# Shift and scale applied to the transposed inputs, per channel, in the first stage of a two-block model kernel

## What is computed

```python
sh1, sc1, gt1, sh2, sc2, gt2 = jnp.split((silu(c) @ w_mod + b_mod)[:, None, :], 6, axis=-1)
csh1, csc1, cgt1, csh2, csc2, cgt2 = jnp.split(silu(c_ctx) @ w_mod + b_mod, 6, axis=-1)
h  = rms_norm(x,   g_pre_mix) * (1.0 + sc1)  + sh1      # 256 latent tokens
hc = rms_norm(ctx, g_pre_mix) * (1.0 + csc1) + csh1     # 256 context tokens
mix, mix_c = token_mix(h, hc, w_in, ...)                # begins with h @ w_in, hc @ w_in
```

## Time and profile before

| | us |
|---|---|
| median of 3 runs | 2170.5 |
| lowest, highest | 2169.6, 2174.39 |
| the profiled execution's own time | 2179.26 |
| its span in the trace | 2177.5 |
| PE busy | 1751.4 |
| DVE busy | 480.1 |
| ACT busy | 352.3 |

### The profile page before, as it was taken

How to read it: one execution, slowest core, us unless ns; L and a number is a source line. 1 busy time by engine, 2 the same in 40 slices (tenths; PEclk the granted TensorE clock), 3 DMA queues, 4 the chain that set the end, 5 groups by cost and what they waited for, 6 DMA issues and landing times. The chain is left out here.

```text
span 2177.5 us, 29445 instructions
## 1 busy us (share of the span) xinstructions
PE 1751.4 (80%) x13116; PEld 1154.2 (53%) x13116; DVE 480.1 (22%) x919; ACT 352.3 (16%) x804; POOL 80.0 (4%) x85
## 2 busy tenths in 40 slices
PE   5999889869969575566555689869999789869997
PEld 1665468749843331122111357638874566558863
DVE  2005363363320400000000143510000144310000
ACT  2110213332311210000000224310000124210000
POOL 0000013213200000000000000000000000000000
PEclk9999889969979687888777889989999889979999
DMA  9321120000016699999999632122354412123340
GB/s 394 140 111 49 62 78 3 3 1 3 4 50 243 260 390 428 428 428 428 427 428 427 263 116 78 69 106 110 149 222 150 173 71 112 40 97 154 155 193 19
DMA packets 35714, 384.53 MB, mean 177 GB/s; under 512 B 6467, under 2 KB 9923, under 8 KB 12803
## 3 DMA queue, kind: packets, MB, share of 16 engines
q1 hardware_dynamic: 35588, 382.65, 43.3%
HBM read 381.59 MB, written 1.05 MB: 176 GB/s over the span
## 5 line engine op out<-in xcount | busy, mean ns | idle before, releaser
L2530 PE MATMUL psum<-arena,weight_ring 128*128 128x256 f32 x1408 | 307.0, 381 | 1.4 <-ACT arena L2559 1.4
L2530 PEld LDWEIGHTS psum<-arena,weight_ring 128*128 128x128 f32 x1408 | 269.2, 191 | 39.0 <-ACT arena L2559 2.0
L1722 PE MATMUL psum<-weight_ring,arena 128*32 128x512 f32 x640 | 142.9, 716 | 126.5 <-DMA arena<-in_w_moe 92.5
L1148 PE MATMUL psum<-arena 64*64 64x64 f32 x4608 | 152.6, 224 | 19.6 <-PEq L905 7.4
L1148 PEld LDWEIGHTS psum<-arena 64*64 64x64 f32 x4608 | 144.6, 139 | 27.8 <-issue 23.4
L2541 PE MATMUL psum<-weight_ring,arena 128*128 128x512 f32 x352 | 151.4, 592 | 0.0
L1722 PEld LDWEIGHTS psum<-weight_ring,arena 128*32 128x32 f32 x640 | 36.0, 129 | 205.0 <-issue 205.0
L1722 PE MATMUL psum<-arena 128*32 128x512 f32 x384 | 109.1, 730 | 36.2 <-DMA weight_ring<-in_w_moe 35.8
L1999 PE MATMUL psum<-arena,weight_ring 128*128 128x256 f32 x512 | 125.7, 407 | 1.4 <-ACT arena L2237 1.4
L1999 PEld LDWEIGHTS psum<-arena,weight_ring 128*128 128x128 f32 x512 | 104.6, 207 | 19.2 <-ACT arena L2237 2.0
L2541 PEld LDWEIGHTS psum<-weight_ring,arena 128*128 128x128 f32 x352 | 66.9, 190 | 83.3 <-issue 83.2
(11 more groups left out here) (453 smaller groups left out, 1977.2 us busy)
## 6 DMA issues: line engine op xcount, KB each, us to landing
weight_ring<-in_w_moe SPq DMA_DIRECT2D x60, 2048.0 KB, 20.5
arena<-in_w_moe SPq DMA_DIRECT2D x36, 2048.0 KB, 20.1
weight_ring<-in_w_in SPq DMA_DIRECT2D x23, 2048.0 KB, 9.0
weight_ring<-in_w_mod SPq DMA_DIRECT2D x12, 2048.0 KB, 8.8
weight_ring<-in_w_gate SPq DMA_DIRECT2D x12, 2048.0 KB, 12.6
weight_ring<-in_w_up SPq DMA_DIRECT2D x12, 2048.0 KB, 8.2
weight_ring<-in_w_down SPq DMA_DIRECT2D x12, 2048.0 KB, 10.4
weight_ring<-in_w_out SPq DMA_DIRECT2D x6, 2048.0 KB, 8.3
```

The costliest lines, as they stand in the source:

```text
L1148: last = nc.tensor.matmul(K.ps[half[d], bank, column + HD * n:column + HD * n + HD], lhs(d, h), rhs(d, h), start=True, stop=True, skip_gro ...
L1722: last = nc.tensor.matmul(K.ps[strip(j), 4, :], xsT[:, k, CAP * e:CAP * e + CAP], ws[j][:, k, :], start=(k == 0), stop=(k == KT - 1), skip ...
L2530: last = nc.tensor.matmul(K.ps[:, f % 4, T * i:T * i + T], w[:, k, at:at + P], hT[:, k, :], start=(k == 0), stop=(k == KT - 1))
```

## The change

The modulation is kept per channel and applied after the transposition, where a channel is a partition:

- DVE makes `h` as the input times the inverse root only (one operation for each tile), PE transposes that, and the half tiles are copied to `K.hT` by DVE (channels 0 to 511) and ACT (512 to 1023) in turns.
- `combine` takes `part` as the stationary side and the two selecting columns as the moving one, in four blocks of 128 channels: its result is 128 channels x 2 conditions for each block, 8 numbers for each partition in all.
- DVE copies the 8 shifts, or makes the 8 scales `(1 + scale) * gain`, and then DVE (11 pieces) and ACT (5 pieces) apply `K.hT = K.hT * scale + shift` in place to pieces of 128 channels x 256 tokens.
- The order of the pieces of `w_mod` is now shift and scale of channels 0 to 511, then shift and scale of 512 to 1023. The first piece is loaded ahead of the inputs. The gain comes as 128x8 numbers (4 KB).
- On PE the transposes now stand between the second and the third part of the modulation.

The diff (removed runs of the three engine programs are cut; they stand in full above):

```diff
--- before.py
+++ after.py
@@ -30,7 +30,7 @@
 
 
 STREAM = (
-    [("w_mod", i) for i in range(4)]
+    [("w_mod", i) for i in (0, 2, 1, 3)]
     + [("w_in", i) for i in (0, 1, 2, 3, 4, 8, 6, 7, 5)]
     + [("w_mod", 4), ("w_mod", 5), ("w_out", 0), ("w_out", 1)]
     + [("w_mod", i) for i in range(6, 12)]
@@ -170,31 +170,22 @@
     cT = A.temp(KT * 2)
     cond = A.temp(KT, 32)
     part = A.temp(2, 512)
-    gain = A.temp(D)
+    gain = A.temp(KT)
     brow = A.temp(2 * D)
-    gmod = A.temp(2, D)
-    shift = A.temp(2, D)
+    gmod, shift = A.temp(KT, 2), A.temp(KT, 2)
+    sumsq, rstd, ms, root = (A.temp(4) for _ in range(4))
+    columns = [i for name, i in STREAM[:4]]
+    tile = lambda j: x_ctx[:, j, :] if j < 2 else x_lat[:, j - 2, :]
+    piece = lambda n: K.hT[:, 4 * (n % 2):4 * (n % 2) + 4, P * (n // 2):P * (n // 2) + P]
+    turned = lambda n: K.ps[:, 4 + n % 4, :].rearrange("p (k t) -> p k t", t=P)
+    by = ["dve", "act"]
...
@@ -202,8 +193,9 @@
             def _(sp):
                 sp.dma_start(cT, K.dram["cT"]).then_inc(in_small, 16)
                 sp.dma_start(brow[0:1, :], K.dram["b_mod"][:, 0:2 * D]).then_inc(in_small, 16)
-                sp.dma_start(gain, K.dram["norm_gains"][0, :].partition_broadcast(P)).then_inc(in_small, 16)
+                sp.dma_start(gain, K.dram["norm_gain_columns"]).then_inc(in_small, 16)
                 sp.dma_start(K.ident, K.dram["ident"]).then_inc(in_small, 16)
+                W.load_to(sp, 1)
                 sp.dma_start(x_ctx, K.dram["ctx"].rearrange("(t p) d -> p t d", p=P)).then_inc(in_x, 16)
                 sp.dma_start(x_lat, K.dram["x"].rearrange("(t p) d -> p t d", p=P)).then_inc(in_x, 16)
                 W.load_to(sp, NB)
@@ -218,95 +210,139 @@
                 for i in range(2):
                     nc.gpsimd.memset(K.head_ones[i * HD:(i + 1) * HD, i * HD:(i + 1) * HD], 1.0).then_inc(ones_set, 1)
 
+            @block.tensor
+            def _(pe):
+                pe.wait_ge(in_small, 64)
+                pe.wait_ge(ones_set, 4)
+                pe.wait_ge(cond_ready, 2)
+
+                def partial(c):
+                    if c >= 2:
+                        pe.wait_ge(part_kept, c - 1)
+                    at = 512 * columns[c]
+                    partial_modulation(nc, K, K.ps[:, c % 2, :], cond, W.take(pe), brow[0:1, at:at + 512],
+                                       W.used if c else None).then_inc(part_made, 1)
+
+                def combine(c):
+
+                    pe.wait_ge(part_kept, c + 1)
+                    if c >= 2:
+                        pe.wait_ge(mod_kept, c - 1)
+                    for b in range(4):
+                        last = nc.tensor.matmul(K.ps[:, 2 + c % 2, 2 * b:2 * b + 2], part[:, c % 2, P * b:P * b + P], K.sel,
+                                                start=True, stop=True, skip_group_check=True)
+                    last.then_inc(mod_made, 1)
+
+                def turn(j):
+                    pe.wait_ge(h_ready, j + 1)
+                    for q in range(2):
+                        n = 2 * j + q
+                        if n >= 4:
+                            pe.wait_ge(hT_read[by[q]], j - 1)
+                        for k in range(4):
+                            last = nc.tensor.transpose(K.ps[:, 4 + n % 4, P * k:P * k + P],
+                                                       h[:, j, P * (4 * q + k):P * (4 * q + k + 1)], K.ident)
+                        last.then_inc(hT_made, 1)
+
+                partial(0)
+                partial(1)
+                pe.wait_ge(sel_ready, 1)
+                combine(0)
+                combine(1)
+                for j in range(4):
+                    turn(j)
+                partial(2)
+                combine(2)
+                partial(3)
+                combine(3)
+                pe.wait_ge(mod_made, 4)
+                nc.tensor.nop().then_inc(W.used, 1)
+
             @block.scalar
             def _(act):
+                def keep_part(c):
+                    act.wait_ge(part_made, c + 1)
+                    if c >= 2:
+                        act.wait_ge(mod_made, c - 1)
+                    nc.scalar.activation(part[:, c % 2, :], K.ps[:, c % 2, :], ACT.Copy).then_inc(part_kept, 1)
+
+                def scale(k, s):
+                    to = K.hT[:, k, T * s:T * s + T]
+                    nc.scalar.activation(to, to, ACT.Identity, bias=shift[:, k, s:s + 1], scale=gmod[:, k, s:s + 1])
+
                 act.wait_ge(in_small, 64)
                 nc.scalar.activation(cT, cT, ACT.Silu).then_inc(silu_done, 1)
+                keep_part(0)
                 act.wait_ge(in_x, 32)
                 for j in range(4):
...
+                    nc.scalar.activation(h[:, j, :], tile(j), ACT.Square, accum_out=sumsq[:, j:j + 1]).then_inc(squares, 1)
                 act.wait_ge(ms_ready, 1)
                 nc.scalar.activation(root, ms, ACT.Sqrt).then_inc(root_ready, 1)
...
+                keep_part(1)
+                for n in range(1, 8, 2):
+                    act.wait_ge(hT_made, n + 1)
+                    nc.scalar.activation(piece(n), turned(n), ACT.Copy).then_inc(hT_read["act"], 1)
+                keep_part(2)
+                act.wait_ge(hT_read["dve"], 4)
+                act.wait_ge(mod_kept, 2)
+                scale(3, 0)
+                scale(3, 1)
+                keep_part(3)
+                act.wait_ge(hT_read["act"], 4)
+                act.wait_ge(mod_kept, 4)
+                for k, s in ((6, 1), (7, 0), (7, 1)):
+                    scale(k, s)
 
             @block.vector
             def _(dve):
                 link = chain(dve, dve_step)
+
+                def keep_modulation(c):
+                    dve.wait_ge(mod_made, c + 1)
+                    half = slice(4 * (c // 2), 4 * (c // 2) + 4)
+                    src = K.ps[:, 2 + c % 2, 0:8].rearrange("p (b s) -> p b s", s=2)
+                    if c % 2 == 0:
+                        nc.vector.tensor_copy(shift[:, half, :], src).then_inc(mod_kept, 1)
+                    else:
+                        nc.vector.scalar_tensor_tensor(gmod[:, half, :], src, 1.0, gain[:, half].unsqueeze(2).broadcast_to([P, 4, 2]),
+                                                       ALU.add, ALU.mult).then_inc(mod_kept, 1)
+
+                def scale(k, s):
+                    to = K.hT[:, k, T * s:T * s + T]
+                    nc.vector.tensor_scalar(to, to, gmod[:, k, s:s + 1], shift[:, k, s:s + 1], ALU.mult, ALU.add)
+
+                def keep_turned(j):
+                    dve.wait_ge(hT_made, 2 * j + 1)
+                    nc.vector.tensor_copy(piece(2 * j), turned(2 * j)).then_inc(hT_read["dve"], 1)
+
                 dve.wait_ge(silu_done, 1)
                 for s in range(2):
...
+                    nc.vector.tensor_copy(cond[:, :, 16 * s:16 * s + 16],
+                                          cT[:, KT * s:KT * s + KT].unsqueeze(2).broadcast_to([P, KT, 16])).then_inc(cond_ready, 1)
                 nc.vector.tensor_reduce(K.sel, K.ident.rearrange("p (k i c) -> p i c k", i=2, c=16)[:, :, 0, :], AX,
                                         ALU.add).then_inc(sel_ready, 1)
                 dve.wait_ge(squares, 4)
                 nc.vector.tensor_scalar(ms, sumsq, 1.0 / D, EPS, ALU.mult, ALU.add).then_inc(ms_ready, 1)
                 dve.wait_ge(root_ready, 1)
                 link(nc.vector.reciprocal(rstd, root))
...
                 for j in range(4):
...
+                    nc.vector.tensor_scalar(h[:, j, :], tile(j), rstd[:, j:j + 1], None, ALU.mult).then_inc(h_ready, 1)
+                    if j:
+                        keep_turned(j - 1)
+                keep_turned(3)
+                keep_modulation(0)
+                keep_modulation(1)
+                dve.wait_ge(mod_kept, 2)
+                dve.wait_ge(hT_read["dve"], 4)
+                for k in range(3):
                     for s in range(2):
...
+                        scale(k, s)
+                keep_modulation(2)
+                keep_modulation(3)
+                dve.wait_ge(mod_kept, 4)
+                dve.wait_ge(hT_read["act"], 4)
+                for k, s in ((4, 0), (4, 1), (5, 0), (5, 1), (6, 0)):
+                    scale(k, s)
     A.high = top
 
 
@@ -2669,6 +2705,7 @@
     a["ident"] = np.eye(P, dtype=np.float32)
     a["b_mod"] = f["b_mod"]
     a["norm_gains"] = f["norm_gains"][0]
+    a["norm_gain_columns"] = f["norm_gains"][0, 0].reshape(KT, P).T
     a["w_mod"] = slots(f["w_mod"][0])
     wi = f["w_in"][0]
     at = np.cumsum([0, 512, 512, 512, 64, 64, 64, 128, 128])
```

More of the change, by code:

```diff
@@ L223, in _ @@
                 act.wait_ge(in_small, 64)
                 nc.scalar.activation(cT, cT, ACT.Silu).then_inc(silu_done, 1)
+                keep_part(0)
                 act.wait_ge(in_x, 32)
                 for j in range(4):
-                    src = x_ctx[:, j, :] if j < 2 else x_lat[:, j - 2, :]
```

(24 more changed lines are left out.)

65 lines of the change are left out of this document (6 added, 59 removed).

## The result

| | before | after |
|---|---|---|
| median, us (19 runs each) | 2172.08 | 2160.7 |
| lowest, highest | 2166.57, 2176.94 | 2153.42, 2171.66 |
| ratio, 95% interval | | 0.9947 (0.9933 to 0.9961) |
| profiled execution: span | 2177.5 | 2155.8 |
| projections begin in its trace | 58.99 | 49.28 |

The change makes the kernel 11.4 us faster on the median. The forecast was 10.9 us faster.

A forecast was written before the change was run, and what follows sets the result against it. It took the first stage as one chain, from w_mod's landing through PE, ACT's root and DVE, to projections at 58.99 us. Its terms summed to 48.1, a gain of 10.9: 2170.5 to 2159.6 us, range 2153 to 2167.5.

The forecast's parts named there:

- Landing: Transfers at the start: first piece of w_mod lands at 11.0 us (bounds 10 to 12.5), inputs 16.0, second piece 20.9.
- PE, first half: Modulation parts 0 and 1 at the low clock with a 4.5 us wait between, then two combinations, done at 29.6 us.
- The norm, hidden: Squares, root and h beside PE's first half: 0.85 to 1.28 us per h, first two by 26, 3.6 us of cover.
- Transposes: Four tiles on PE between parts 1 and 2: 6.9 us, 29.6 to 36.5, or 35.7 if the clock rises.
- PE, second half: Parts 2 and 3, each with copy and combination, at full clock: 4.5 us each, 9.0 for both, ending at 44.7.
- rival (1): Clock drops between parts 2 and 3: part 3 costs 2.56 us more, its combination 0.75; gain 7.6, 2162.9; chance 0.17.
- DVE's end: Behind PE's last combination: one read of eight scales and five applications of 0.411 us, about 2.5 in all, to 47.2.
- Ring: Weight queue: slots come free before it empties, five pieces up to 36 us; projections find their pieces landed.
- Rival (2): Clock stays low through transposes and second half: projections begin at 55.5 us, gain 3.5, 2167.0; chance 0.10.
- Rival (5): More gain: projections keep the full clock, saving 1.5 us, or the first piece lands at 10: 2157; chance 0.08.
- (3): Gain given back where PE waits 44.8 us for expert weights, if their stream's start does not move: about 2170; chance 0.04.
- (4): Slower: five more clock falls in the rest, up to 3.4 us each, turn the gain into 4.3 loss: 2175; chance 0.04.

The follow-up runs named there:

- root_early: The kernel before, with ACT's root moved directly behind the sums of squares: projections begin at 52.83 us, median 2169.85 us, ratio 0.9982.
- turn_last: The changed kernel with transposes, copies and applications behind all four modulation parts: projections begin at 49.89 us, median 2163.94 us, ratio 0.9969.
- first_piece_behind: The changed kernel with the first piece of w_mod loaded behind both inputs again: projections begin at 49.06 us, median 2159.32 us, ratio 0.9946.
- second trace: The changed kernel profiled again with no edit: projections begin at 44.34 us.
- kept_busy_sized: Changed kernel, two pieces ahead of inputs, part 2 before transposes, combinations 2 and 3 behind part 3, useless PE products in waits: 2152.87 us, ratio 0.9907.

## Why the prediction was right, point by point

- *What bounds it:* right. The chain through ACT's root and DVE's 16 operations was the end of the stage, and it is gone. The gain of 9.7 us is a net: from the last combination's end to the projections it is 2.78 us instead of 17.66, and that end itself came 5.17 later (46.50 against 41.33), mostly since the transposes and the pause of 4.46 now stand ahead of it. root_early gives about 3.4 of the 9.7 to the root's place, and turn_last some 2 to the transposes' place. The per-channel form alone has no experiment; its share is read from the rows.
- *Landing:* 10.82 against 11.0, the second piece 20.73 against 20.9. The step behind it, that the first piece's early start buys little, was in the sum (the pause of 4.5 us, measured 4.46) but I did not name it as a part of the change without effect on PE. first_piece_behind shows it.
- *PE, first half:* part 1 ended and the combinations began at 26.14 (26.3); the two combinations took 3.4 us (1.7 each), as taken. At the full clock one takes 1.05 with its tail, not 0.95.
- *The norm, hidden:* one `h` took 0.747 us, below my cheap end of 0.85: I had doubled the 0.427 of a copy of half the length, and these two rows suggest a part that doesn't grow with the length (of two different operations, so this is not shown). It did not matter: two were there at 24.3, against 29.58.
- *Transposes:* 29.58 to 35.57, against 29.6 to 35.7. The clock rose among them.
- *PE, second half:* here the size was off. I took 9.0 us, and it was 11.0 (35.50 to 46.50), since rival (1) came in: part 3 ran at the low clock from 41.09. That cost 1.7 us and not the 2.56 and 0.75 priced there, since its bias and its combination still ran at full speed. In the second trace the second half took 9.3 (32.24 to 41.55). So whether rival (1) comes in is not decided by the program but differs between its executions.
- *DVE's end:* 1.9 us against 2.5. One application is 0.408 us long, as priced (0.411), but I set them end to end, and in a row they overlap: five took 1.70, so one begins every 0.32. ACT's are 0.589 each (I had 0.476), three took 1.58, and they stayed hidden.
- *End of the stage:* 0.83 against 0.84. *Ring:* PE waited for no third, fourth or later piece in the first 50 us. The queue did run low for want of a free slot (220 GB/s from 39.13 to 40.10), where I had said that it would not; nothing waited for it.
- *The sum:* projections at 49.28 against 48.1 in the first trace, 44.34 and 49.11 in the others. The median moved by 11.4 against 10.9. That the two agree so well is luck: the clock makes this stage 5 us longer or shorter, and no trace of the changed kernel took the forecast's path whole. Two had the late rise that I assumed and rival (1) with it, the third had no fall but a rise before the transposes, which I had not listed.
- *The rule of the Trainium skill* ("TensorE: Matmul & The Clock Gate", Part 4, PE-mode transpose), that transposes do not bring the full clock, did not hold here. In the changed kernel they are the only work on PE between 29.58 and 35.50, and part 2 behind them ran at full speed (2.8 us, against 5.4 for part 1). There 2-column products came ahead of them; in the kernel before, PE had been idle for 6.85 us, and the clock rose among them as well.
- *Rival (2):* not seen; the second half was not at half speed, and the projections began 6 us ahead of its 55.5. *Rival (5):* not seen; the first piece landed at 10.82, and the projections started at the low clock. kept_busy_sized shows its mechanism when the pause is filled (3.73 us for the first product). *Rivals (3) and (4):* not seen. The sum of (4) is wrong: five falls of 3.4 us are 17.0, a loss of 6.1 and not 4.3. The rest of the kernel varied by 13 us with the same instructions, more than the 4.8 us that I took from three runs. That I had too small: the changed kernel's runs span 18 us.

One cost I left out: the projections start at the low clock behind a pause of 2.78 us, and their first product took 6.45 us, against 5.27 before (58.99 to 64.26). That hands back 1.2 of the 9.7 us. In the second traces of both kernels it was 6.43 against 5.47.

## What to carry to other kernels

Look at where an operation stands in its engine's program before changing its form: the root behind the fourth copy cost 3.4 us, and moving it needed no new layout. When a transfer is pulled ahead, ask what the consumer waits for next; an earlier first piece gave PE nothing here, since the second landed when it did. In a stage where PE waits for transfers, its idle time is paid a second time in the work that follows, and products of no use, sized by their measured duration, brought the last 2.5 us at the start of the projections and 1.7 in the first product behind it. On the median they brought 3.4 us, at intervals that still overlap.

## What the runs showed of the hardware

- The same program had its first stage end at 44.34 or at 49.28 us, by where the clock rose: at the end of part 1 in one execution, only among the transposes in two others. With PE filled from 4.69 us on, part 0 at 10.80 already ran at full speed.
- PE did nothing but combinations with 2 columns, a one-row bias and a pause of 0.74 us between dense products, and the clock fell in three of four traces with the changed kernel's order. How much each of the three counts for is open: no run separated them.
- The part of the kernel behind the first stage takes 2105 to 2119 us with the same instructions. Between the first two traces it is PE's clock (1720.8 against 1709.5 us busy), and within each kernel's runs the shorter ones have the higher mean clock (0.896 against 0.885 at the two ends of the changed kernel's). What moves the clock between executions was not tried. This part is the larger share of the spread of the runs.
